# Delta rule's triangular inverse: the untransposed factor rebuilt by transposes of the transposed one, in three steps a level

## Reference, cut to what matters

```python
def chunk_gated_delta_rule(q, k, v, g, beta):
    ...
    a = jnp.einsum("bhncd,bhnsd->bhncs", k_beta, k) * decay
    t_mat = jnp.eye(C, dtype=jnp.float32) + jnp.where(strict, a, 0.0)
    rhs = jnp.concatenate([v_beta, k_beta * jnp.exp(g)[..., None]], axis=-1)
    sol = lax.linalg.triangular_solve(t_mat, rhs, left_side=True, lower=True, unit_diagonal=True)
    ...
def hybrid_mixer(xn, w_in, ...):
    ...
    o = chunk_gated_delta_rule(q, k, v, g, beta)
    o = rms_norm_2(o, dn_norm_g) * jax.nn.silu(z.reshape(hd).astype(jnp.float32))
    ...
    c = causal_depthwise_conv(c, cf_dw_w) + cf_dw_b
    c = jax.nn.silu(layer_norm(c, cf_ln_g, cf_ln_b))
    return jnp.concatenate([o, c], axis=-1) @ w_out
```

## Time and profile before

| | us |
|---|---|
| median of the three runs shown | 2673.62 |
| the profiled execution's own time | 2671.96 |
| its span (first to last instruction) | 2670.2 |
| TensorE busy | 2611.9 (98%) |
| VectorE busy | 1627.5 (61%) |
| ScalarE busy | 1353.3 (51%) |

### The profile page before, as it was taken

How to read it: one execution, slowest core, us unless ns; L and a number is a source line. 1 busy time by engine, 2 the same in 40 slices (tenths; PEclk the granted TensorE clock), 3 DMA queues, 4 the chain that set the end, 5 groups by cost and what they waited for, 6 DMA issues and landing times. The chain is left out here.

```text
span 2670.2 us, 31500 instructions
## 1 busy us (share of the span) xinstructions
PE 2611.9 (98%) x12544; PEld 2168.4 (81%) x12544; DVE 1627.5 (61%) x1992; ACT 1353.3 (51%) x1916; POOL 0.2 (0%) x4
## 2 busy tenths in 40 slices
PE   8999999999999999998899999999999999999998
PEld 7877888888888887887888887888888888888886
DVE  6685555555555556567887856644555555555555
ACT  5554544444444446578867644444544444444443
POOL 0000000000000000000000000000000000000000
PEclk9999999999999999999999999999999999999999
DMA  6533665556655654654443327544465566556553
GB/s 219 159 135 134 219 191 192 188 188 190 192 188 187 190 194 151 199 167 157 129 165 113 133 95 267 175 157 143 162 207 189 185 191 194 187 184 192 195 188 134
DMA packets 235241, 468.70 MB, mean 176 GB/s; under 512 B 8187, under 2 KB 17110, under 8 KB 233814
## 3 DMA queue, kind: packets, MB, share of 16 engines
q1 hardware_dynamic: 234806, 466.16, 53.5%
q10 hardware_dynamic: 288, 0.52, 0.1%
HBM read 460.36 MB, written 6.29 MB: 175 GB/s over the span
## 5 line engine op out<-in xcount | busy, mean ns | idle before, releaser
L138 DVE TENSOR_TENSOR WL<-Wt,WH 128x1024 fp32r<-128x1024 f32 (+1 forms) x862 | 1041.7, 1210 | 802.8 <-ACT WH L135 744.1
L135 ACT ACTIVATE WH<-Wt 128x1024 fp32r<-128x1024 f32 (+1 forms) x862 | 898.7, 1046 | 802.7 <-PE ps L168 797.4
L168 PE MATMUL ps<-WH,XT 128*128 128x512 f32 (+1 forms) x3392 | 1087.8, 394 | 4.6 <-DVE WL L138 4.3
L168 PE MATMUL ps<-WH,HT 128*128 128x512 f32 (+2 forms) x3392 | 1059.7, 389 | 2.5 <-DVE WL L138 2.5
L168 PEld LDWEIGHTS ps<-WH,XT 128*128 128x128 f32 x3392 | 638.6, 189 | 136.8 <-DVE WL L138 5.1
L168 PEld LDWEIGHTS ps<-WH,HT 128*128 128x128 f32 x3392 | 636.2, 188 | 128.3 <-DVE WL L138 3.5
L168 PE MATMUL ps<-WL,XT 128*128 128x512 f32 (+1 forms) x1696 | 660.0, 389 | 0.0
L168 PE MATMUL ps<-WL,HT 128*128 128x512 f32 (+2 forms) x1696 | 655.0, 386 | 0.0
L168 PEld LDWEIGHTS ps<-WL,XT 128*128 128x128 f32 x1696 | 320.3, 189 | 62.5 <-issue 1.0
L168 PEld LDWEIGHTS ps<-WL,HT 128*128 128x128 f32 x1696 | 319.7, 189 | 61.5 <-issue 1.0
L138 DVE TENSOR_TENSOR H<-H,ps 128x512 f32<-128x512 f32 x144 | 92.5, 683 | 26.7 <-PE ps L168 26.7
(11 more groups left out here) (262 smaller groups left out, 1301.8 us busy)
## 6 DMA issues: line engine op xcount, KB each, us to landing
Wt<-in_mlp_w SPq DMA_DIRECT2D x128, 1024.0 KB, 5.3
Wt<-in_w_up SPq DMA_DIRECT2D x64, 1024.0 KB, 5.4
Wt<-in_w_down SPq DMA_DIRECT2D x64, 1024.0 KB, 5.0
Wt<-in_w_in SPq DMA_DIRECT2D x53, 1024.0 KB, 5.1
Wt<-in_w_out SPq DMA_DIRECT2D x32, 1024.0 KB, 5.1
Wt<-in_xa_wk SPq DMA_DIRECT2D x16, 1024.0 KB, 5.1
Wt<-in_xa_wv SPq DMA_DIRECT2D x16, 1024.0 KB, 5.0
Wt<-in_xa_wq SPq DMA_DIRECT2D x16, 1024.0 KB, 5.0
```

Source lines behind the costliest of these rows:

```text
L135: return self.p.act.do(lambda e: e.activation(out, in_, func, **kw), w, self.name + "_a")
L138: return self.p.dve.do(lambda e: e.tensor_tensor(out, a, b, op), w, self.name + "_v")
L168: return self.p.pe.do(lambda e: e.matmul(out, l, r, start=start, stop=stop), w, self.name + "_t" if sig else None)
```

## The change

At the levels 2, 4, 8, 16 and 32 the M update by four matmuls and one VectorE subtraction for each group of four heads goes. After the MT update comes a new `yield`; then the new MT of each head is transposed on TensorE, ScalarE copies the result over M, and another `yield` follows. At level 64 nothing but the place of the assignment changes. A level has three steps in place of two (level 64 still two), so everything in `gen_delta` behind the first block moves five halves later and everything behind the second block ten.

```diff
                 for hb in range(2):
                     hs = slice(4 * hb, 4 * hb + 4)
-                    if lev != LEVELS[-1]:
-                        bi, bk, bf = banks.get()
-                        for i in range(4):
-                            h = 4 * hb + i
-                            t = st.mm(bk[:, i * P:(i + 1) * P], MT[:, h, :], PP[:, h, :], t_p[hb], t_mt[hb], bf,
-                                      sig=(i == 3))
-                        nm[hb] = st.tt(M[:, hs, :], M[:, hs, :], h3(bk), SUB, t, t_m[hb])
-                        banks.free(bi, nm[hb])
                     bi, bk, bf = banks.get()
...
                 p_free = t
+                yield
+                if lev != LEVELS[-1]:
+                    for hb in range(2):
+                        hs = slice(4 * hb, 4 * hb + 4)
+                        bi, bk, bf = banks.get()
+                        for i in range(4):
+                            t = st.tr(bk[:, i * P:(i + 1) * P], MT[:, 4 * hb + i, :], ident, nt[hb], bf, sig=(i == 3))
+                        nm[hb] = st.act(M[:, hs, :].rearrange("p h c -> p (h c)"), bk, ACT.Copy, t, t_p)
+                        banks.free(bi, nm[hb])
+                    yield
                 t_m, t_mt = nm, nt
-                yield
```

## The result

The changed kernel takes 2656.66 us (median of 6 runs, 2654.64 to 2658.3), the kernel before on the same chips 2672.76 us (6 runs, 2672.04 to 2673.64). The ratio is 0.994, with a 95% interval of 0.9929 to 0.995: 16.1 us less, beside a forecast of 2657. The profiled execution took 2657.37 us, 14.6 less than that of before, of which the code ahead of the change, which is the same, took back about 1 us: the first `gen_delta` row on VectorE stood at 1349.7 us in the trace before and stands at 1350.7 now.

A forecast was written before the change was run, and what follows sets the result against it. TensorE, busy 98% of the span, was taken as the bound. From the profiled 2671.96 us, minus 9.0, minus 8.2, plus 0.7 gave 2655.5; the runs' median lies 1.66 higher, so 2657 was forecast, range 2651 to 2668.

The forecast's parts named there:

- Term 1: TensorE in the inverse's levels: eight transposes replace eight small products, 0.90 us less per level, 9.0 us in all.
- Term 2: VectorE and ScalarE in the levels: 20 fewer subtractions, 20 more copies; covered by TensorE, so costed at nothing.
- Term 3: End of the second block: waits for WL and VT go with their slow clock, 8.2 us; late weight load costs nothing.
- Term 4: Level 2 waits for VectorE stay in both blocks; `gen_ln`'s first matmuls newly wait 0.7 us for the convolution's last addition.
- Rival A: Second block's end: gaps stay or return elsewhere, only the TensorE saving pays, 2664.6 us, up to 2668; chance 0.18.
- Rival B: Levels: ScalarE becomes the bound and its M copies wait, 35 us more, 2692 us; chance 0.10.
- Rival C: Levels: transposes lower the clock, costing 18 us over ten groups, 2675 us, no change; chance 0.05.
- Rival D: Second block: the wait at level 2 goes as well, 4.8 us, giving 2652 us; chance 0.07.

The follow-up runs named there:

- XV later: The changed kernel with the second 2 MB transfer (XV) sent eight halves later: 2655.41 us, ratio 0.9937 to the kernel before.

## Why the prediction was right

**Term 1 (9.0 us) held.** The changed kernel and the one with the steps alone differ by little but the exchange, and by 9.9 us in their medians (8.7 in the profiled executions from level 1's transposes on); eight transposes more cost 0.87 us a level, beside the 0.85 that the prediction read from level 1 in the earlier trace rows.

**Term 2 (nothing) held.** ScalarE was reckoned at 12.1 of 12.8 us a level; in the five levels of the first block it is busy between 10.2 us (of 12.66, 1395.43 to 1408.09) and 12.4 (of 12.86, 1420.74 to 1433.60), 11.5 in the mean. Doubling the copies cost at most some 2.4 us, and moving them to VectorE nothing that shows. The half between update and transposes, named there as the cover, is worth more than the prediction's 0.7 us of lateness suggests: without it the waits are some 12 us.

**Term 3 (8.2 us) was right in its mechanism, and one step of it failed.** The waits for WL and VT went, and with them the low clock at 1616; the steps alone do that, so it is the order. The failed step is the one on what is late next: of the weight load behind XKB and XV, "so this costs nothing to 3.9 us; I take nothing, as in the row". It cost 1.7 us of waiting for H and 1.8 us of slow clock, 3.5 us in the profiled execution. In the run with VectorE's copies the same wait did not bring the slow clock, so the cost is 1.7 to 3.5 us. The prediction followed the weight split alone, which has halves in reserve, and not what is queued behind it on VectorE. In the earlier trace rows ScalarE's wait was 3.9 us with no evacuation behind it; now it is 5.35 with one.

**Term 4 was too careful.** The second block's wait was kept whole; it shrank from 3.0 to 2.3 us, and the clock did not fall behind it in the profiled execution (1.8 us; it did in others). The 0.7 us taken for `gen_ln`'s first matmuls do not show: in the timeline they follow B·M without idle time. Together 0.7 + 1.8 + 0.7 = 3.2 us, which about make up for the 3.5. That these cancel is luck: the sum came nearer than its parts.

Rival A did not come: no wait for WL beside LNA rows. Rival B needed ScalarE on the path for 17 us; the doubled copies bound it at 2.4. Rival C is excluded by the doubled transposes at a clock of 1.00; the Trainium skill's statement (TensorE: Matmul & The Clock Gate, Part 4: PE-mode transpose) that transposes don't count as busy for the clock in the way that matmuls do shows no effect here in groups of 8 or 16 between matmuls (1.00 at 1400 to 1420). Rival D came in part: the second block's wait at level 2 shrank by 0.7 us and did not go.

What stays open is how much of the difference between versions within 3 us of each other is the clock. The same wait was followed by the low clock in one execution and not in another, and five runs don't separate these versions.

## What to carry to other kernels

Where one engine is full, an exchange of its work for a cheaper operation pays by the distance between starts in the trace, but only if the wait that comes with it is covered: here the same exchange gained some 9 us with a half of other work in between and cost 5 to 8 us without it. Moving a chain of background work is a change of its own; look at what it no longer meets (some 6 us here), and at each queue for what it newly meets. Of a late transfer, follow not only its reader but everything queued behind that reader on the next engine.

## What was not expected of the hardware

An f32 transpose of 128x128 costs half of an f32 product of the same size on TensorE's queue: 0.85 to 0.87 us for eight against 1.70 for eight. And the granted clock fell to its lower level in some executions behind gaps as short as 1.7 us in all (0.91 at 1660 to 1680 in the profile after), while a gap of 2.3 us at 1510 left it at 1.00 there and not in the run with XV later. This is one source of the spread between executions of one kernel, some 4 us here (2654.64 to 2658.3). Another part of it lies ahead of the change: in the profiled executions level 1's first transposes begin anywhere from 1378.83 us (copies by VectorE) to 1382.39 (exchange alone), behind the same program.
